# Residual halves one place on, maxima in the second chunk, and U's second head copied by VectorE

## The reference

```
h = rms_norm(x);  z = h @ w_in
rwkv:  r, k, v, decay, a, gate from z (token-shifted);  16 heads x 64
       state = state * w_t + (state @ a_t) b_t^T + v_t k_t^T;  y_t = state @ r_t     for each t
       y = (group_norm(y) + bonus) * gate
attention: 8 heads x 128, rotary, causal softmax (one block of 256 keys holds all)
x += rms_norm(concat(y, attention) @ w_out)
x += rms_norm(square(relu(rms_norm(x) @ w_up)) @ w_down)
```

## Time and profile before

| what | value |
| --- | --- |
| median of 3 runs | 2487.6 us (2487.11 to 2488.59) |
| the profiled execution | 2488.29 us, of which its span is 2486.4 us |
| TensorE, busy | 2455.4 us |
| VectorE, busy | 1681.4 us |
| ScalarE, busy | 1252.2 us |
| mean granted TensorE clock | 0.998 of full speed |

### The profile page before, as it was taken

How to read it: one execution, slowest core, us unless ns; L and a number is a source line. 1 busy time by engine, 2 the same in 40 slices (tenths; PEclk the granted TensorE clock), 3 DMA queues, 4 the chain that set the end, 5 groups by cost and what they waited for, 6 DMA issues and landing times.

```text
span 2486.4 us, 47886 instructions
## 1 busy us (share of the span) xinstructions
PE 2455.4 (99%) x15931; PEld 2060.0 (83%) x15931; DVE 1681.4 (68%) x2809; ACT 1252.2 (50%) x2048; POOL 129.6 (5%) x186
## 2 busy tenths in 40 slices
PE   8999999999999999999999999999999999999998
PEld 7888888788888888888788888877888888888887
DVE  6778877576566566466578888885765565664665
ACT  6555655464344344344455565555553443443443
POOL 3000100000000000000011111100000000000000
PEclk9999999999999999999999999999999999999999
DMA  7444444655656555665554444445556656566564
GB/s 211 138 121 120 138 135 125 196 184 187 195 182 194 193 183 193 195 186 187 160 147 126 128 120 135 126 126 199 182 179 201 183 190 194 178 196 193 184 194 152
DMA packets 437963, 420.06 MB, mean 169 GB/s; under 512 B 19566, under 2 KB 352000, under 8 KB 437888
## 3 DMA queue, kind: packets, MB, share of 16 engines
q1 hardware_dynamic: 434240, 412.55, 53.4%
q0 software_dynamic: 3648, 6.52, 0.9%
HBM read 416.90 MB, written 2.10 MB: 169 GB/s over the span
## 4 chain that ended last, share of the span: by engine, by line
PE 97%; DVE 1%; ACT 1%; DMA 1%; issue 0%; SPq 0%; POOL 0%; DVEq 0%; POOLq 0%
PE gemm_bank L538 33%; PE gemm_bank L539 18%; PE gemm_bank L565 11%; PE gemm_bank L566 11%; PE gemm_bank L567 11%; PE gemm_bank L541 2%; PE mix_banks L718 1%; PE mix_banks L725 1%; PE mix_banks L689 1%; PE mix_banks L760 1%; PE mix_banks L766 1%; PE mix_banks L765 1%; PE mix_banks L756 1%; PE mix_banks L590 0%; PE mix_banks L661 0%; PE mix_banks L659 0%
## 5 line engine op out<-in xcount | busy, mean ns | idle before, releaser
L1228 DVE TENSOR_TENSOR b_wlo<-b_raw,b_whi 128x1024 fp32r<-128x1024 f32 x777 | 944.7, 1225 | 533.0 <-ACT b_whi L923 531.9
L538 PE MATMUL gemm_bank<-b_hT,b_whi 128*128 128x512 f32 x3420 | 1248.5, 405 | 1.7 <-DVE b_hT L1280 1.1
L923 ACT ACTIVATE b_whi<-b_raw 128x1024 fp32r<-128x1024 f32 x777 | 810.3, 1056 | 624.0 <-PE gemm_bank L567 414.2
L539 PE MATMUL gemm_bank<-b_hT,b_wlo 128*128 128x256 f32 x3648 | 1011.7, 281 | 0.0
L538 PEld LDWEIGHTS gemm_bank<-b_hT,b_whi 128*128 128x128 f32 x3420 | 643.3, 188 | 154.6 <-issue 7.3
L539 PEld LDWEIGHTS gemm_bank<-b_hT,b_wlo 128*128 128x128 f32 x3648 | 689.7, 189 | 9.8
L565 PE MATMUL gemm_bank<-b_whi,b_mT 128*128 128x512 f32 x1280 | 501.4, 392 | 0.7 <-DVE b_wlo L1228 0.7
L567 PE MATMUL gemm_bank<-b_whi,b_mT 128*128 128x512 f32 x1280 | 498.3, 389 | 0.0
L566 PE MATMUL gemm_bank<-b_wlo,b_mT 128*128 128x512 f32 x1280 | 498.3, 389 | 0.0
L565 PEld LDWEIGHTS gemm_bank<-b_whi,b_mT 128*128 128x128 f32 x1280 | 240.4, 188 | 50.3 <-ACT b_whi L923 1.1
L567 PEld LDWEIGHTS gemm_bank<-b_whi,b_mT 128*128 128x128 f32 x1280 | 240.3, 188 | 50.0
(11 more groups left out here) (234 smaller groups left out, 1776.3 us busy)
## 6 DMA issues: line engine op xcount, KB each, us to landing
b_raw<-in_w_up SPq DMA_DIRECT2D x256, 512.0 KB
b_raw<-in_w_down SPq DMA_DIRECT2D x256, 512.0 KB
b_raw<-in_w_in SPq DMA_DIRECT2D x384, 256.0 KB
b_raw<-in_w_out SPq DMA_DIRECT2D x60, 512.0 KB
b_raw<-in_w_in SPq DMA_DIRECT2D x8, 512.0 KB
b_xt<-in_x SPq DMA_DIRECT2D x8, 256.0 KB, 5.3
b_raw<-in_w_out SPq DMA_DIRECT2D x8, 256.0 KB
out<-b_xt SPq DMA_DIRECT2D x8, 256.0 KB, 2.4
```

Of the source, the lines that this page charges most:

```text
L538: mm(bank[b0 + b][:, :], whi[r][:, cols], pair, start=first, stop=False)
L539: m = mm(bank[b0 + b][:, 0:SEQ], wlo[r][:, cols], act[:, kt, 0, :], start=False, stop=False)
L923: f(whi[r][:, :], raw[r][:, :, :].rearrange("p a b -> p (a b)"), ACT.Copy).then_inc(hi_done, 1)
L1228: tt(wlo[r][:, :], flat(raw[r][:, :, :]), whi[r][:, :].bitcast(F32), ALU.subtract).then_inc(lo_done, 1)
```

## The change

The high and residual halves of the turn stand one place further on in the lists of ScalarE and VectorE: what was done at the place of step j is now done one place earlier in the turn, for the steps from 2 on. On VectorE the place behind the rotary sum (`step(5)`) is now `step(6)` and stands behind the copy of U in chunk 0; chunk 1 has none; `step(7)` stands at the end of chunk 3, ahead of the addition of Y, where it stood behind it.

ScalarE copies U's first head only. VectorE copies the second, in a new function `second_u`, in each chunk. The causal mask, the maxima and their scaling move on VectorE from chunk 2 to chunk 1, and the exponentials on ScalarE with them, behind `finish(1)`. The reciprocal of the sums comes after the state of chunk 2, and the scaling of the probabilities into chunk 3. The key shifts and the key square move with them. TensorE's list, GpSimd's and SyncE's are the same.

```diff
@@ ScalarE, mixer @@
                 step(1)
+                step(2)
                 act.wait_ge(e["turned"], V)
...
-                step(2)
                 step(3)
+                step(4)
                 for lv in range(1, LEVELS):
...
                     if lv == 2:
-                        step(4)
+                        step(5)
...
                     if lv == 4:
-                        step(5)
-                    if lv == 5:
                         step(6)
...
-                    for h in range(2):
-                        hs = slice(HEAD * h, HEAD * h + HEAD)
-                        f(VU[opp(c), c, hs], mb[3][hs, 256 + HEAD * h:256 + HEAD * h + HEAD], ACT.Copy).then_inc(e["u_out"], 1)
+                    f(VU[opp(c), c, 0:HEAD], mb[3][0:HEAD, 256:320], ACT.Copy).then_inc(e["u_out"], 1)
                     if c == 0:
                         step(7)
                     if c == 1:
                         finish(1)
-                    if c == 2:
 
                         act.wait_ge(e["nmax"], V)
@@ VectorE, mixer @@
                 step(1)
+                step(2)
...
-                step(5)
...
+                def second_u(c):
+
+                    dve.wait_ge(e["u_sum"], NCH * n + c + 1)
+                    nc.vector.tensor_copy(VU[opp(c), c, HEAD:P], mb[3][HEAD:P, 320:384]).then_inc(e["u_out"], 1)
...
+                    if c == 0:
+                        second_u(c)
+                        step(6)
...
                     if c == 1:
-                        step(6)
-                    if c == 2:
 
                         dve.wait_ge(e["score_sum"], V)
                         tt(sm[:, :], mb[2][:, 0:384], cst[:, C_CAUS:C_CAUS + 384], ALU.add).then_inc(e["masked"], 1)
+                        second_u(c)
...
+                    if c == 2:
+                        second_u(c)
+                        if more:
+                            key_shift(l, i + 1, n + 1, 0)
...
+                    if c == 2:
+
+                        dve.wait_ge(e["expd"], 2 * n + 2)
+                        nc.vector.reciprocal(small[:, 14:16], small[:, 12:14]).then_inc(e["rsum"], 1)
+                        if more:
+                            key_shift(l, i + 1, n + 1, 1)
+                    if c == 3:
+
+                        second_u(c)
+                        dve.wait_ge(e["rsum"], V)
+                        ts(sm[:, 0:P], sm[:, 0:P], small[:, 14:15], None, ALU.mult)
+                        ts(sm[:, P:3 * P], sm[:, P:3 * P], small[:, 15:16], None, ALU.mult).then_inc(e["probs"], 1)
+                        if more:
+                            key_square(l, i + 1, n + 1)
+                        step(7)
+
                 dve.wait_ge(e["y_sum"], V)
...
-                step(7)
```

More of the change, by code:

```diff
@@ L1431, in mixer @@
                 merge(0, 1, mb[3][:, 0:P]).then_inc(e["z_ready"], 1)
-                step(2)
+                step(3)
                 for lv in range(1, LEVELS):
@@ L1439, in mixer @@
                     if lv == 2:
-                        step(3)
+                        step(4)
                     if lv == 3:
```

## The result

The changed kernel takes 2498.56 us (median of 6, 2497.78 to 2499.25), the kernel before 2488.55 us on the same chips (median of 6). The ratio is 1.0041, 95% interval 1.003 to 1.0051. The forecast was 2500, range 2492 to 2507. The profiled executions differ by 10.8 us in span, 2486.4 to 2497.2, at granted clocks of 0.998 and 0.997.

A forecast was written before the change was run, and what follows sets the result against it. TensorE, busy 99% of the span, was taken as the bound. 14 loop turns at 0.84 us (11.8) and two last turns (0.8) made +12.6 us on 2488.3: 2500.9, 2500.2 after the median correction, stated as 2500, range 2492 to 2507.

The forecast's parts named there:

- Chunk 0: First chunk: VectorE's state queues behind the copy of U and the residual, so its reader's load starts 0.42 us late.
- Chunks 1 and 2: Middle chunks: VectorE's state comes later, so the loads that read it start 0.48 and 0.18 us late.
- U: State matmul's weight load in all four chunks: no more waiting for ScalarE's copy, 0.11 us gained each, 7.0 us in all.
- Early residuals: Residual halves moved one place on, up to the level stage: they fall into idle time and cost nothing.
- The queue in order: VectorE's first in, first out queue: neither residual nor state can pass the copy of U; otherwise 2497.
- the one behind U of chunk 3: End of turn, main term: key norms lose 0.49 us; the load turning the normalised Y starts 0.81 us late.
- Now VectorE copies to s + 0.32: Chunk 3, s being when U's sum is ready: copy taken as 0.28 us, then scaling to s + 0.90.
- The Trainium skill's 0.19 us for the copy: VectorE's copy of U from PSUM, alternative estimate: stalls behind a copy 0.09 us shorter each, sum some 1.5 us smaller.
- The last turns: Last pair of each layer, without key work: reduction 0.38 us late, 0.4 us lost each, 0.8 together.
- U's gain alone: Rival: Y's late addition and chunk 0's state stay hidden, only the quicker copy of U counts; 2478 to 2481, chance 0.11.
- become the bound round the loop: Rival: VectorE's lateness passes into the next turn and grows, 1.3 us or more a turn; 2507 to 2512, chance 0.06.

The follow-up runs named there:

- the experiment: Changed kernel with chunk 0 as before: ScalarE copies both heads of U there, VectorE's residual stands ahead of the chunks; 2490.76 us.
- the version with the probabilities first: Changed kernel with chunk 0 as before and, in chunk 3, probabilities ahead of the copy of U, key square behind it; 2482.82 us.

## Why the prediction was right, and what was mis-sized

**Sign, places and mechanism** held. *Chunk 0*: 0.42 forecast, 0.46 in the rows, 0.45 by the experiment. That this is so close is partly luck: with the 0.22 added, the residual ended at 85.89, sooner than the 85.94 of the forecast, but the state did not start 0.06 us ahead of its end, as forecast, but 0.02 behind it (85.91 against 85.88). *Chunks 1 and 2*: 0.48 and 0.18 forecast for the next readers, 0.46 and 0.22 in the rows. (The terms shown for chunk 1 add up to 89.78, not 89.7; the forecast does not say that the state starts some 0.08 us ahead of the scaling's end, as it does in the kernel before.) *U*: the waits went, and the two passes of the state matmul take 0.38 us again where they took 0.49. *Early residuals*: nothing forecast, nothing measured. *The queue in order*: putting the state ahead of the residual moved the stall and did not remove it.

**The term that was too large** is the one behind U of chunk 3. The step "Now VectorE copies to s + 0.32" took a copy of 0.28 us from the state operations and let the next instruction begin only after it. The copy took 0.23 us and the next instruction began 0.15 us after the copy's start (94.21, 94.36). So everything behind it came 0.16 to 0.21 us sooner than forecast: the key square was seen 1.18 us after U's sum instead of 1.37 (the key norms waited 0.27 us, not 0.49), and the normalised Y ended at s + 5.88 instead of s + 6.05 (s is 94.17 here). The turning of Y was then 0.64 us late in the first turn instead of 0.81, and the turns are longer by 0.62 us in layer 0 and 0.56 in layer 1 instead of 0.84. Why layer 1 loses less is not shown. The Trainium skill's 0.19 us for the copy ("VectorE: DVE Perf Modes", The TRN2 errata) is 0.04 us too low, the row that I took 0.05 too high. With 0.19 the sum would have been 11.1, nearer to the 10.0 measured. But of the 0.16 us by which the next instruction came sooner, the shorter copy is 0.05, and 0.11 is its start before the copy's end, which neither figure holds.

**The sum**: 7 x 0.62 + 7 x 0.56 = 8.3 us in the loops. The last turns are 0.31 and 0.39 us longer up to the turning of Y (0.4 forecast), so some 9 of the 10.8 us between the profiled spans have a place. The stretch from the first product of layer 0's last turn to that of layer 1's first turn scatters from 885.1 to 888.2 us over the kernels of the table, so the rest stays unplaced.

**What was not seen**: in the kernel before, a tick behind the probabilities waited for the last residual, which the waits book as issue (7.3 us in 22 waits; 2.7 in 8 in the changed kernel). One of them, in the first turn:

```profile
97.61 0.19 PEld L538 LDWEIGHTS gemm_bank<-b_hT,b_whi 128*128 128x128 f32 x1 [0.34 <-issue]
```

The change took these waits away, a gain that the prediction did not list. TensorE was 0.40 us late at the key norms and, with that wait gone, only 0.13 late at attention's product (line 792, 98.92 against 99.01, with the 0.22). It bought nothing, since Y ended the stall behind it.

**The rivals.** U's gain alone needed slack behind chunk 3, and there was none beyond the 0.06 us read from the earlier trace rows: the turning of Y waits in all 16 turns. VectorE did not become the bound round the loop: each turn of the changed kernel loses about the same (50.35 to 50.49 us in layer 0), and the loss does not grow from turn to turn.

## What to carry to other kernels

- A copy split over two engines is done when the later one is, and the second engine's own queue waits with it: what stands behind the wait, in each chunk, belongs in the price. Here putting chunk 0 back gave 0.45 us a turn, and with the key square ahead too, taking the other three copies off VectorE gave another 0.15, against a gain of 0.11 us for each copy.
- Before a stall is moved by reordering, look whether the engine has the free time at all before the next consumer; if not, the stall turns up one place on, as chunk 0's did (0.80 us at the state's reader, then 0.70 at U of chunk 1).
- Work that waits for nothing goes into the idle time in front of the wait, not behind it: the key square moved ahead of the copy gave 0.37 us a turn.

## Hardware behaviour that was not expected

VectorE's copy of 64x64 float32 from PSUM took 0.23 us in all chunks, against 0.28 to 0.29 for one state operation of the same size with a scalar per partition (0.60 for two). How soon the next instruction follows depended on the chunk. The changed kernel's chunks 1 and 2:

```profile
87.85 0.23 DVE L1471 COPY b_VU<-mix_banks 64x64 f32<-64x64 f32 x1
87.99 0.27 DVE L1491 TENSOR_REDUCE b_small<-b_sm 128x1 f32<-128x128 f32 x1
...
91.12 0.23 DVE L1471 COPY b_VU<-mix_banks 64x64 f32<-64x64 f32 x1
91.38 0.48 DVE L1333 SCALAR_TENSOR_TENSOR b_sh<-b_kf,b_prm,b_zt 128x256 f32<-128x256 f32 x1
```

In chunks 1 and 3, where the copy writes partitions 0 to 63, the next one (128 partitions) began 0.14 to 0.15 us after its start; in chunks 0 and 2, where it writes 64 to 127, 0.26 us after it, when the copy was over. That holds in every turn of every kernel here in which the next instruction did not wait for another engine. It is not the kind of the next instruction: behind chunk 0's copy a residual began 0.26 us after it (84.18, 84.44), and in the last turns of the version with the probabilities first, where a residual stands behind chunk 3's copy, 0.15:

```profile
440.78 0.23 DVE L1473 COPY b_VU<-mix_banks 64x64 f32<-64x64 f32 x1 [0.18 <-PE mix_banks L760]
440.93 1.21 DVE L1226 TENSOR_TENSOR b_wlo<-b_raw,b_whi 128x1024 fp32r<-128x1024 f32 x1
```

The Trainium skill ("VectorE: DVE Perf Modes", Two Vector instructions with no wait between them) gives, as a model, that an instruction whose output starts in another quadrant (32 partitions) than the last output into the same memory starts only when all earlier ones have finished. The traces agree in all four chunks; no kernel here changed the partitions alone to test it.
